# Odd layer of a hybrid encoder: the projection matmuls are spread over all four steps of a half, and the gate is taken at a half's end

## What is computed

```python
def window_gqa_with_sink(q, k, v, sink, cos, sin):
    ...
        s = jnp.einsum('bqhgd,bkhd->bhgqk', qx, kx, preferred_element_type=jnp.float32) * scale
        ...
        m = jnp.maximum(jnp.max(s, axis=-1, keepdims=True), sink_g)
        p = jnp.exp(s - m)
        p = p / (jnp.sum(p, axis=-1, keepdims=True) + jnp.exp(sink_g - m))
        return jnp.einsum('bhgqk,bkhd->bqhgd', p.astype(vx.dtype), vx)
...
def odd_layer(x, norm_w, w_in, w_out, sink, cos, sin):
    h = rmsnorm(x, norm_w)
    proj = jnp.einsum('bsd,de->bse', h, w_in)
    qc, kc, vc, gc = split_cols(proj, ODD_SIZES)
    oc = window_gqa_with_sink(qc, kc, vc, sink, cos, sin) * jax.nn.silu(gc)
    return jnp.einsum('bse,ed->bsd', oc, w_out)
```

## Time and profile before

| | |
|---|---|
| median of 3 runs | 1174.91 us (1174.14 to 1177.41) |
| the profiled execution | 1174.97 us, of which 1173.0 us is the span from first to last instruction |
| busy share of the span | PE 97%, DVE 83%, ACT 57% |
| odd layer's first head | about 739 to 789 us |
| 13 half steps of heads 1 to 7 | about 789 to 1128 us, 26.04 us each |
| hand-written tail | about 1128 us to the end |

### The profile page before, as it was taken

How to read it: one execution, slowest core, us unless ns; L and a number is a source line. 1 busy time by engine, 2 the same in 40 slices (tenths; PEclk the granted TensorE clock), 3 DMA queues, 4 the chain that set the end, 5 groups by cost and what they waited for, 6 DMA issues and landing times. The chain is left out here.

```text
span 1173.0 us, 18575 instructions
## 1 busy us (share of the span) xinstructions
PE 1137.7 (97%) x5750; PEld 916.2 (78%) x5750; DVE 970.8 (83%) x1912; ACT 672.7 (57%) x1310; POOL 0.2 (0%) x4
## 2 busy tenths in 40 slices
PE   6999999999999999999999999999999999999996
PEld 5877778778778778778787867778888888888876
DVE  6879789789879879878878898778888888888886
ACT  6475564554654654654664655366665565666653
POOL 0000000000000000000000000000000000000000
PEclk9999999999999999999999999999999999999998
DMA  7514423324224125125215211643232433323111
GB/s 212 154 52 104 130 72 71 109 72 94 84 72 121 57 72 138 43 70 143 61 46 144 89 37 44 153 115 91 54 89 54 107 82 98 91 54 89 54 37 72
DMA packets 131817, 103.59 MB, mean 88 GB/s; under 512 B 5441, under 2 KB 116417, under 8 KB 131777
## 3 DMA queue, kind: packets, MB, share of 16 engines
q1 hardware_dynamic: 131776, 103.07, 32.3%
HBM read 77.88 MB, written 2.10 MB: 68 GB/s over the span
## 5 line engine op out<-in xcount | busy, mean ns | idle before, releaser
L74 PE MATMUL bank_proj<-hH,w_hi 128*128 128x512 f32 x856 | 343.7, 402 | 1.2 <-issue 1.2
L76 PE MATMUL bank_proj<-hH,w_lo 128*128 128x512 f32 x856 | 335.0, 391 | 0.0
L75 PE MATMUL bank_proj<-hL,w_hi 128*128 128x512 f32 x856 | 334.5, 391 | 0.0
L76 PEld LDWEIGHTS bank_proj<-hH,w_lo 128*128 128x128 f32 x856 | 160.9, 188 | 35.3
L74 PEld LDWEIGHTS bank_proj<-hH,w_hi 128*128 128x128 f32 x856 | 161.5, 189 | 32.3 <-issue 1.9
L75 PEld LDWEIGHTS bank_proj<-hL,w_hi 128*128 128x128 f32 x856 | 161.5, 189 | 30.4 <-issue 0.5
L1907 ACT ACTIVATE probs<-bank_odd_score,small 128x256 f32<-128x256 f32 (+1 forms) x128 | 66.3, 525 | 56.1 <-DVE small L2145 56.0
L1914 ACT ACTIVATE probsT<-bank_odd_turn 128x256 fp32r<-128x256 f32 (+1 forms) x128 | 49.0, 434 | 85.5 <-PE bank_odd_turn L1638 85.4
L1196 DVE TENSOR_TENSOR w_lo<-w_raw,w_hi 128x1024 fp32r<-128x1024 f32 x74 | 89.4, 1216 | 9.6 <-ACT w_hi L703 9.5
L703 ACT ACTIVATE w_hi<-w_raw 128x1024 fp32r<-128x1024 f32 x74 | 77.9, 1054 | 29.4 <-DMA w_raw<-in_w_in_even 28.9
L759 ACT ACTIVATE probs<-bank_score,small 128x512 f32<-128x512 f32 x64 | 43.4, 684 | 63.2 <-DVE small L1039 57.2
(11 more groups left out here) (403 smaller groups left out, 2203.1 us busy)
## 6 DMA issues: line engine op xcount, KB each, us to landing
w_raw<-in_w_in_even SPq DMA_DIRECT2D x72, 512.0 KB, 4.9
w_raw<-in_w_in_odd SPq DMA_DIRECT2D x36, 512.0 KB, 4.4
qs<-parts SPq DMA_DIRECT2D x96, 128.0 KB, 2.3
ks<-parts SPq DMA_DIRECT2D x40, 256.0 KB, 4.2
o_raw<-in_w_out_even SPq DMA_DIRECT2D x15, 512.0 KB, 6.4
o_raw<-in_w_out_odd SPq DMA_DIRECT2D x14, 512.0 KB, 6.4
out<-w_raw SPq DMA_DIRECT2D x8, 256.0 KB, 2.1
mixT<-in_x SPq DMA_DIRECT2D x2, 512.0 KB, 5.4
```

The lines of the kernel that those rows point to most:

```text
L74: pe.matmul(out, hi, moving_hi, start=start, stop=False)
L75: pe.matmul(out, hi, moving_lo, start=False, stop=False)
L76: return pe.matmul(out, lo, moving_hi, start=False, stop=stop)
```

## The change

Nothing is computed differently and no instruction is added or taken away; places in the order of PE and DVE change.

- In `half_step` on PE, the first two steps of a half now hold 6 projection groups each in place of 8, and the last two steps, which held only output tiles, hold 2 each. `proj(h, n)` ends in the second step, ahead of `values(h, half, 0)`, and `proj(h, n + 1)` ends in the fourth. `values` stands in the middle of each step's filling.
- In `first_head`, three groups of projection 0 come before `scores(0, 0, 0)`, and the other groups are dealt out anew.
- On DVE, `scale_gate` of a half goes from the third step (after the first `add_out`) to the end of the fourth, behind the last `low` and ahead of the last `add_out`.

```diff
--- before.py
+++ after.py
@@ -1689,48 +1689,44 @@
                 proj(0, -2)
                 proj(0, -1)
                 turn_values(1)
+                proj(0, 0, 0, 3)
                 pe.wait_ge(ready.sem, ready.at(0, 3))
                 pe.wait_ge(k_moved.sem, k_moved.at(0, 4))
                 scores(0, 0, 0)
-                proj(0, 0, 0, 4)
+                proj(0, 0, 3)
                 pe.wait_ge(v_kept.sem, v_kept.at(0, 2))
                 turns(0, 0, 0)
                 scores(0, 0, 1)
-                proj(0, 0, 4)
+                proj(0, 1, 0, 4)
                 values(0, 0, 0, 0)
-                proj(0, 1, 0, 2)
                 turns(0, 0, 1)
                 scores(0, 0, 2)
-                proj(0, 1, 2, 5)
+                proj(0, 1, 4)
                 values(0, 0, 1, 0)
-                proj(0, 1, 5)
                 turns(0, 0, 2)
                 scores(0, 0, 3)
-                proj(0, 2, 0, 3)
+                proj(0, 2, 0, 5)
                 values(0, 0, 2, 0)
-                proj(0, 2, 3, 6)
 
                 turns(0, 0, 3)
                 pe.wait_ge(k_moved.sem, k_moved.at(0, 8))
                 scores(0, 1, 0)
-                proj(0, 2, 6)
+                proj(0, 2, 5)
+                proj(0, 3, 0, 2)
                 values(0, 0, 3, 0)
-                proj(0, 3, 0, 3)
                 turns(0, 1, 0)
                 scores(0, 1, 1)
                 turn_weight(0, 0, turn_of(1, False))
-                proj(0, 3, 3)
+                proj(0, 3, 2)
                 values(0, 1, 0, 0)
                 turns(0, 1, 1)
                 scores(0, 1, 2)
-                proj(0, 4, 0, 2)
+                proj(0, 4, 0, 4)
                 values(0, 1, 1, 0)
-                proj(0, 4, 2, 4)
                 turns(0, 1, 2)
                 scores(0, 1, 3)
-                proj(0, 4, 4, 6)
+                proj(0, 4, 4)
                 values(0, 1, 2, 0)
-                proj(0, 4, 6)
 
             def half_step(h, half, group, group_before, last):
 
@@ -1738,24 +1734,28 @@
                 before, h_before = 1 - half, (h if half else h - 1)
                 turns(h_before, before, 3)
                 scores(h, half, 0)
-                proj(h, n, 0, 4)
+                proj(h, n, 0, 3)
                 values(h_before, before, 3, group if half else group_before)
-                proj(h, n, 4, 8)
+                proj(h, n, 3, 6)
                 turns(h, half, 0)
                 scores(h, half, 1)
                 turn_weight(h_before, before, turn_of(half, True))
+                proj(h, n, 6, 8)
+                values(h, half, 0, group)
                 proj(h, n + 1, 0, 4)
-                values(h, half, 0, group)
-                proj(h, n + 1, 4, 8)
                 turns(h, half, 1)
                 scores(h, half, 2)
                 out_tile(h, 4 * half, 5 * half + 2)
+                proj(h, n + 1, 4, 5)
                 values(h, half, 1, group)
+                proj(h, n + 1, 5, 6)
                 out_tile(h, 4 * half + 1, 5 * half + 3)
                 turns(h, half, 2)
                 scores(h, half, 3)
                 out_tile(h, 4 * half + 2, 5 * half + 4)
+                proj(h, n + 1, 6, 7)
                 values(h, half, 2, group)
+                proj(h, n + 1, 7, 8)
                 out_tile(h, 4 * half + 3, 5 * half + 5)
 
             def iteration(h, group, group_before, last=False):
@@ -2284,8 +2284,6 @@
                 out(0)
                 if last:
                     low(h, 3)
-                if not zeroth:
-                    scale_gate(h, 2 * half + 2, 1 - half, use)
                 add_halves(h, half, 0)
                 out(1)
                 maxima(h, half, 3)
@@ -2300,8 +2298,8 @@
                     low(h, 6)
                 if first:
                     scale_gate(0, 1, 0)
-                elif zeroth:
-                    scale_gate(h, 4, 0, use)
+                else:
+                    scale_gate(h, 2 * half + 2, 1 - half, use)
                 out(3)
 
             def iteration(h, zeroth, last):
```

## The result

| | median us | lowest to highest |
|---|---|---|
| before | 1175.64 (4 runs, the profiled one among them) | 1174.14 to 1177.41 |
| changed | 1185.80 (4 runs, the profiled one among them) | 1181.62 to 1186.26 |

The ratio is 1.0081, with a 95% interval from 1.0064 to 1.0097: slower by 0.8%. The profiled execution is the 1181.62 us one, the quickest of the four, with a span of 1179.6 us.

What follows compares the result with a forecast made beforehand. PE, busy 97% of the span, was taken as the bound. On 1174.97 us, +9.1 + 0.6 - 0.3 - 3.1 = +6.3 gave 1181.3, and +5.1 for three half-speed clock stretches gave 1186 us; range 1179 to 1193.

Steps and rivals of the forecast that it cites:

- The main step: Half 0, heads 1 to 7: PE waits 2.1 us for `low_y` at the first tile; +1.3 us seven times, +9.1.
- Half 1: Half 1, heads 1 to 6: new PE waits replace old ones; +0.1 us a half, +0.6 in all, bounds -0.3 and +0.4.
- Head 0: Regrouped first head: two long PE waits filled or shortened; 3.1 us won, bounds 1.5 and 3.6.
- The first wait: Head 0, PE's 1.94 us wait for the first queries at 741.40: filled by three groups taking 2.05 us.
- the waits of 0.4 and 1.7 us: Head 0: the 1.98 us wait at 780.03 shrinks to 0.4, and PE runs dry about 1.7 at the next `turns`.
- The idle time of DVE at 764.71: Head 0: DVE's one large idle time, 2.18 us, claimed to go as PE comes early.
- The gate: `scale_gate` moved to a half's end: costs nothing in the halves, 0 to -0.4 us before the tail, taken as -0.3.
- The clock: Seven new 2.1 us PE waits: three followed by 1.2 GHz stretches of about 1.7 us, +5.1; bounds 0 and +12.
- +5.1: Clock loss after the new waits in half 0: three half-speed stretches of about 1.7 us each.
- +6.3: Whole kernel without clock loss: +9.1 half 0, +0.6 half 1, -0.3 gate, -3.1 head 0, giving 1181.3 us.
- the clock stays at 2.4 GHz: Rival, heads 1 to 7: same new PE waits but no clock loss, 1181.3 us; chance 0.15.

Runs made afterwards that it cites:

- experiment 1: Changed kernel with PE's order in half 0 of heads 1 to 7 put back as before; 1169.04 us, ratio to before 0.9949.
- experiment 4: Changed kernel with `low_y(h - 1, 1)` moved between `rotate` and `part` on DVE in half 0; 1171.87 us, ratio to before 0.9973.
- experiment 5: Changed kernel with 9 extra throwaway matmuls ahead of the first output tile in half 0; 1176.45 us, ratio to before 1.0015.
- experiment 6: Changed kernel with 14 instead of 12 projection groups ahead of the first output tile in half 0; 1173.24 us, ratio to before 0.9982.
- experiment 2: Kernel before with only the changed kernel's `first_head` order; 1171.02 us, ratio to before 0.9965.
- experiment 7: Changed kernel with `low_y` between `rotate` and `part`, and half 0's groups 13 ahead of the first tile, then 1, 1, 1; 1168.54 us, ratio 0.9940.
- experiment 3: Kernel before with only the two `scale_gate` edits; 1175.41 us, ratio to before 0.9999.
- experiment 8: Experiment 7's kernel with the first `add_out` of a half ahead of `maxima(h, half, 2)` on DVE; 1174.84 us, ratio to before 0.9995.

## Why the prediction was right, and where only its sum was

**The main step.** The forecast had PE at the first tile 2.7 us earlier, `low_y` where it was, and so a wait of 2.1 us. The wait was there in all seven heads (2.01 us as the trace draws it), `low_y` ended at 15.98 in the half shown, and half 0 took 27.29 us against 27.4 forecast. The term was +9.1 forecast and 7 x 1.25 = +8.8 measured (the last half 0, which ends in the tail, lost somewhat less). Experiments 1, 4, 5 and 6 show it as the cause.

**Half 1** was mis-sized: +0.6 forecast, and 6 x (25.62 less 26.04) = -2.5 measured, outside the bound of -0.3 a half. The forecast held that DVE's 0.72 us of idle time is all that can go, and added new waits of PE for `low_turn` and `add_out`; PE's list above shows no such rows. DVE's timeline of a changed half 1 (it starts at 867.17):

```profile
873.32 1.23 DVE L2216 TENSOR_TENSOR w_lo<-w_raw,w_hi 128x1024 fp32r<-128x1024 f32 x1
874.62 0.76 DVE L2152 TENSOR_TENSOR probsT<-bank_odd_turn,probsT 128x256 fp32r<-128x256 f32 x2
...
881.93 1.01 DVE L2152 TENSOR_TENSOR probsT<-bank_odd_turn,probsT 128x384 fp32r<-128x384 f32 x2
```

`low_turn(h, 1, 1)` starts 14.76 after the half's start, where it was 16.06 (935.43 in the earlier trace rows less the half's start at 919.37 in the earlier trace rows): 1.3 us earlier. A second idle time of DVE, ahead of `low_turn(h, 1, 0)`, went too, since PE's transposes were there when ACT came to them. In the kernel before it was 0.43 us:

```profile
927.31 0.76 DVE L2152 TENSOR_TENSOR probsT<-bank_odd_turn,probsT 128x256 fp32r<-128x256 f32 x2 [0.43 <-ACT probsT L1914]
```

So `values` and the tiles found their inputs sooner than forecast.

**Head 0:** -3.1 forecast. In the two profiles the head ends 3.8 us earlier (785.42 against 789.18), just outside the bound of 3.6. Experiment 2 measured 4.2 for it alone, of which a part may be the tail's stretch that did not fall in. Some 1.7 of the 3.8 us is the stretch at 781, which only the kernel before has there: in experiment 7's profile, with the same waits in head 0 and a stretch behind them, the head takes 45.57 us from its first `scores` (743.00 to 788.57), against 43.91 in the changed kernel (741.51 to 785.42). The first wait went as worked out; the waits of 0.4 and 1.7 us that were forecast came out as 0.6 and 0.8. The idle time of DVE at 764.71 did go, and `low_turn` came 2.6 us earlier, but much of that was given back at `add_halves`, which came only 1.5 us earlier (769.11 before), since ACT had waited for a transfer of weights ahead of its `soft_max`. The forecast had not seen this. The rows of the changed kernel:

```profile
762.08 0.76 DVE L2152 TENSOR_TENSOR probsT<-bank_odd_turn,probsT 128x256 fp32r<-128x256 f32 x2
...
764.05 1.06 ACT L1893 ACTIVATE w_hi<-w_raw 128x1024 fp32r<-128x1024 f32 x1 [0.78 <-DMA w_raw<-in_w_in_odd]
...
767.60 0.42 DVE L2183 TENSOR_TENSOR summed<-bank_odd_out,vt 64x256 f32<-64x256 f32 x1 [1.86 <-ACT vt L1927]
```

**The gate:** the forecast was nothing in the halves and -0.3 us before the tail. Experiment 3 measured no difference in the total, which cannot tell 0.3 us. In the profiles the last half 0, up to the tail's turn of the weights, takes 26.35 us in the kernel before and in experiment 2, and 26.1 and 26.0 us with the gate moved (experiments 3 and 1).

**The clock:** three stretches of 1.7 us were taken, +5.1. The profiled run had four, of 1.5 us each. A typical run lost about 9 us by them, as experiment 5 shows. That the clock could fall was read from rows; how often was a guess from four old waits, within its stated bounds.

So +6.3 and +5.1 became about +2 and +9. The +2 is from the two profiles: the 13 halves take 11.9 us more (350.67 against 338.76), of which 6.2 are the four stretches, and 5.7 less the 3.8 of head 0 is 1.9. With 8.9 for the clock that makes 10.8, where the medians differ by 10.2. The total of 1186 against 1185.8 is right by two errors of opposite sign, and to that extent by luck. The mechanism, the place and the sign were right; the size of the part at full clock was three times too large, by half 1 and head 0, and the clock's part was little more than half of what it cost. Of the rivals, "the clock stays at 2.4 GHz" was priced at 1181.3; experiment 5, which is this case, measured 1176.45, so it would have been almost no change. The loss of this change is mostly a loss of clock.

## What to carry to other kernels

Before a filling (the matmuls that keep PE busy between dependent steps) is evened out, look up for each moved instruction what it waits for beside its own chain. An output tile that moves ahead by 2.7 us needs all its inputs 2.7 us earlier, and its slack was 0.7. A new wait of PE costs its own length less the small waits that it replaces, and in addition what the clock takes, which here was more than four times the net of the other terms. When a wait has been shortened, ask which wait of the same resource comes next; here it was the second and then the third use of one bank, and moving the engine's work from one to the other only lengthened the chain.

## What the runs showed of the hardware that was not expected

- PE's clock was granted at half after the 2.01 us waits in four of seven heads of the profiled run, and the four were heads in succession, one stretch in each half 0. In heads 1 to 7 of the nine other profiles, where no wait of PE was longer than 1.0 us (experiment 8), there was none.
- The same wait in the same code is followed by half speed in one run and not in another. All ten profiles have a wait of 2.4 us at about 106 us and one of 1.6 us in the tail. A stretch stood behind the first in four profiles (experiments 3, 6, 7 and 8) and behind the second in three (the kernel before, experiments 3 and 7). In head 0, waits of 0.64 and 0.79 us some 2 us apart were followed by half speed at 782.5 in experiments 7 and 8 and not in the six other profiles with them; the old order's wait of 2.0 us was followed by it in both profiles that have it (the kernel before, experiment 3). So one profile of a kernel does not tell how many stretches its other runs have. The window behind the first wait, in the kernel before and in experiment 3, with the clock at 1.00 and 0.50:

```profile
106.60:109.40 2.80, 2.80 (x16) 2.33 (x15) 2.77 (x6) 2.01 (x2) 0.00 (x0) 1.00 0.02 6
...
106.60:109.40 2.80, 2.80 (x9) 2.27 (x8) 2.77 (x6) 2.00 (x2) 0.00 (x0) 0.50 0.00 0
```

- Filling the seven waits with matmuls whose results are thrown away bought about 9 us (experiment 5: 1176.45 us against 1185.80), by keeping the clock up.
- A stretch at half speed cost 1.5 us (28.84 less 27.29).
